# Start addresses of fp32r operands, moved off the common point of a 256-byte stretch

## The reference

```
# block 1 (blocks 2 and 3 have other branches and the same outline)
x = layer_norm(ALPHA * x + 0.5 * (silu(x @ w_gate) * (x @ w_up)) @ w_down)      # tags f1, f1d
proj = x @ w_in                                                              # q, k, v, z, xbc, gates
y_attn = attention(q, k, v) @ w_attn_branch                                   # a1_yh, a1_yl
y_ssm  = ssd(...) @ w_ssm_branch                                              # z1_yh, z1_yl
x = layer_norm(ALPHA * x + (gate_a * y_attn + gate_s * y_ssm) @ w_out)        # tag o1
x = layer_norm(ALPHA * x + 0.5 * swiglu(x, ffn2))                             # tags f2, f2d
# block 2: stick-breaking attention (a2), spatial gate (g2), gated linear attention (l2), o2, c2d
# block 3: sparse attention (a3), pools (p3), delta rule (d3), o3, f3 (first projection), f3d
```

## Time and profile before

| | us |
|---|---|
| median of 2 runs | 3423.38 (3421.72 and 3425.03) |
| the profiled execution: span from first to last instruction | 3420.3 |
| outside that span in the two runs (run less span) | 1.4 and 4.7 |
| TensorE busy | 3348.4 (98%), 18576 matmuls |
| VectorE busy | 2278.8 (67%) |
| ScalarE busy | 1593.4 (47%) |

### The profile page before, as it was taken

One profiled execution on the slowest core, in us unless ns is written; L12 is line 12 of the kernel. 1 busy time (PEld: TensorE's weight loads), 2 busy tenths in 40 slices (PEclk: granted clock), 3 DMA queues, 4 the chain that ended last, 5 costly groups with the idle time before them and its releaser, 6 DMA issues. The chain is left out here.

```text
span 3420.3 us, 48737 instructions
## 1 busy us (share of the span) xinstructions
PE 3348.4 (98%) x18576; PEld 2856.2 (84%) x18576; DVE 2278.8 (67%) x3709; ACT 1593.4 (47%) x2932; POOL 339.6 (10%) x375
## 2 busy tenths in 40 slices
PE   8999999999999999999999999999999999999999
PEld 7998888877788899887887888888787888889987
DVE  6887474778447787853565576667465567678865
ACT  3565254454433455555324363346355243355654
POOL 1000200022010100022010100000000104222200
PEclk9999999999999999999999999999999999999999
DMA  6346312220334435520454242245410330142464
GB/s 218 109 149 206 111 49 64 91 69 25 104 102 137 157 108 170 173 73 25 160 161 143 75 134 97 96 165 168 122 38 26 109 99 26 38 148 81 136 200 157
DMA packets 107988, 386.48 MB, mean 113 GB/s; under 512 B 12060, under 2 KB 14764, under 8 KB 107504
## 3 DMA queue, kind: packets, MB, share of 16 engines
q1 hardware_dynamic: 101088, 364.86, 32.6%
q0 software_dynamic: 4528, 16.43, 1.5%
q10 hardware_dynamic: 2144, 2.10, 0.2%
HBM read 379.13 MB, written 4.21 MB: 112 GB/s over the span
## 5 line engine op out<-in xcount | busy, mean ns | idle before, releaser
L445 DVE TENSOR_TENSOR w_low<-ring,w_high 128x1024 fp32r<-128x1024 f32 (+1 forms) x481 | 591.3, 1231 | 496.3 <-ACT w_high L433 490.6
L433 ACT ACTIVATE w_high<-ring 128x1024 fp32r<-128x1024 f32 (+1 forms) x481 | 485.0, 1010 | 491.8 <-PE bank L469 212.8
L469 PE MATMUL bank<-x_low,w_high 128*128 128x512 f32 (+1 forms) x1712 | 654.9, 388 | 19.5 <-DVE w_low L445 13.0
L469 PE MATMUL bank<-x_high,w_low 128*128 128x512 f32 (+1 forms) x1712 | 641.4, 380 | 0.0
L469 PE MATMUL bank<-x_high,w_high 128*128 128x512 f32 (+1 forms) x1712 | 417.8, 381 | 0.0
L469 PEld LDWEIGHTS bank<-x_low,w_high 128*128 128x128 f32 x1712 | 323.1, 189 | 82.4 <-issue 17.6
L469 PEld LDWEIGHTS bank<-x_high,w_low 128*128 128x128 f32 x1712 | 323.4, 189 | 56.9 <-issue 3.6
L469 PEld LDWEIGHTS bank<-x_high,w_high 128*128 128x128 f32 x1712 | 304.6, 189 | 59.1 <-issue 4.8
L738 PE MATMUL bank<-w_low,x_high 128*128 128x512 f32 (+1 forms) x384 | 145.6, 379 | 3.6 <-ACT z_z L2102 1.5
L740 PE MATMUL bank<-w_high,x_high 128*128 128x512 f32 (+1 forms) x384 | 143.5, 374 | 0.0
L739 PE MATMUL bank<-w_high,x_low 128*128 128x512 f32 (+1 forms) x384 | 143.5, 374 | 0.0
(11 more groups left out here) (821 smaller groups left out, 8215.0 us busy)
## 6 DMA issues: line engine op xcount, KB each, us to landing
ring<-in_W SPq DMA_DIRECT2D x686, 512.0 KB, 3.5
X<-in_x POOLq DMA_DIRECT2D x1, 2048.0 KB, 9.7
x_spill<-X POOLq DMA_DIRECT2D x1, 2048.0 KB, 8.2
X<-x_spill POOLq DMA_DIRECT2D x4, 512.0 KB, 3.5
ring<-in_W SPq DMA_DIRECT2D x4, 432.0 KB, 4.0
out<-X SPq DMA_DIRECT2D x3, 512.0 KB, 5.5
const<-in_consts POOLq DMA_DIRECT2D x1, 1133.0 KB, 10.6
f_hid<-in_xT ACTq DMA_DIRECT2D x4, 256.0 KB, 8.2
```

What stands on the lines that cost most here:

```text
L433: ac.activation(b.UH[u.place][:, 0:u.K * u.n], u.src(), ACT.Copy).then_inc(*b.split.act.up("high", i))
L445: dv.tensor_tensor(b.UL[u.place][:, 0:n], u.src(), b.UH[u.place][:, 0:n].bitcast(F32), SUB).then_inc(*b.split.dve.up("low", i))
L469: i = pe.matmul(out, w[:, k, c], v, start=n == 0 and q == 0, stop=last and q == 3 * K - 1)
```

## The change

It gives a `past` of its own to each of these tiles, and leaves all instructions, their order and their waits as they are. One element is 4 bytes, so `past=4` is 16 bytes.

- `cols` (column constants): three lines on, as `const`.
- `x_high` 4 elements on, `x_low` 8.
- Branch inputs: a1 12 and 20, z1 24 and 28 (with `m1_xs`, which has the same place, 24), a2 32 and 36, g2 40 and 44, l2 48 and 52, a3 56 and 60, p3 16 and 2, d3 48 and 6.
- Inputs of the second projections: a table `IN_PAST` with one value for each of a tag's tiles, from 4 to 60. f3d keeps 0.

Tiles behind a moved one are pushed back to their own point, so they stay at the same point of the stretch, 256 bytes further on at most steps.

```diff
--- before.py
+++ after.py
@@ -237,12 +237,12 @@
         self.cl, self.csize = const_layout()
         self.cx = {0: a.take("const", self.csize[0], past=3 * LINE)}
         self.colat, self.ncol = col_at()
-        self.colt = a.take("cols", self.ncol)
+        self.colt = a.take("cols", self.ncol, past=3 * LINE)
         self.MOD, self.GN, self.cond = a.take("MOD", 48), a.take("GN", 2, 8), a.take("cond", 8)
         self.small = a.take("small", 112)
         self.X = a.take("X", 4, 1024)
-        self.XH = a.take("x_high", 8, 512, dtype=F32R)
-        self.XL = a.take("x_low", 8, 512, dtype=F32R)
+        self.XH = a.take("x_high", 8, 512, dtype=F32R, past=4)
+        self.XL = a.take("x_low", 8, 512, dtype=F32R, past=8)
         self.UH = [a.take("w_high", SLOT, dtype=F32R) for _ in range(NU)]
         self.UL = [a.take("w_low", SLOT, dtype=F32R) for _ in range(NU)]
         self.units, self.unit_of, self.key_of, self.n_high, self.n_low = [], {}, [], 0, 0
@@ -755,7 +755,7 @@
     def __init__(self, b, area, tag, nk, src, units=4):
         self.tag, self.nk, self.src, self.n = tag, nk, src, units
         self.tail, self.more, self.added, self.begun = units, {}, [], False
-        self.H = [area.take(f"{tag}_in", 2, 256, dtype=F32R) for _ in range(units)]
+        self.H = [area.take(f"{tag}_in", 2, 256, dtype=F32R, past=p) for p in IN_PAST[tag][:units]]
 
     def used(self, g, i):
         p, k = i // self.nk, i % self.nk
@@ -858,6 +858,7 @@
         x.then_inc(*g.pe.up(d.tag, "part", i))
 
 
+IN_PAST = {"f1d": (4, 8, 12, 16), "o1": (24, 32, 40), "o2": (28, 56, 60), "o3": (36, 44, 52), "f2d": (20, 24, 28, 32), "c2d": (36, 40, 44, 48), "f3d": (0, 0, 0, 0)}
 THIRD = "third tile of tokens done"
 
 
@@ -1507,8 +1508,8 @@
         self.S = [a.take("a1_s", 2, 257) for _ in range(5)]
         self.PT = [a.take("a1_pt", 4, 128) for _ in range(3)]
         self.sm = [a.take("a1_sm", 16) for _ in range(5)]
-        self.YH = a.take("a1_yh", 8, 512, dtype=F32R)
-        self.YL = a.take("a1_yl", 8, 512, dtype=F32R)
+        self.YH = a.take("a1_yh", 8, 512, dtype=F32R, past=12)
+        self.YL = a.take("a1_yl", 8, 512, dtype=F32R, past=20)
         self.units = [(n, j) for n in range(4) for j in range(8)]
         self.ba = Branch(self.gb, "ba1", "w_in", OGA, "w_attn_branch", [[(64 * lo, 64), (64 * hi, 64)] for lo, hi in PAIRS1],
                          Halves(lambda k: self.YH[:, k, :], lambda k: self.YL[:, k, :]), self.merged,
@@ -1517,7 +1518,7 @@
         a = Area(b, at)
         self.gcv, self.gd = Group(b, "conv1"), Group(b, "ssd1")
         xs_at = a.at
-        self.XS = a.take("m1_xs", 4, 2048)
+        self.XS = a.take("m1_xs", 4, 2048, past=24)
         after_xs = a.at
         self.BT = a.take("m1_bt", 4, 512)
         self.CT = a.take("m1_ct", 4, 512)
@@ -1542,9 +1543,9 @@
         self.DT = a.take("m1_dt", 4, 32)
         self.ssd = [(c, g) for c in range(4) for g in range(4)]
         self.yx_at = xs_at
-        self.YXH = Area(b, xs_at).take("z1_yh", 4, 2048, dtype=F32R)
+        self.YXH = Area(b, xs_at).take("z1_yh", 4, 2048, dtype=F32R, past=24)
         a = Area(b, after_xs)
-        self.YXL = a.take("z1_yl", 4, 2048, dtype=F32R)
+        self.YXL = a.take("z1_yl", 4, 2048, dtype=F32R, past=28)
         self.gz = Group(b, "z1")
         self.zt = [a.take("z1_z", 512) for _ in range(2)]
         self.sq = [a.take("z1_sq", 512) for _ in range(2)]
@@ -2333,7 +2334,7 @@
         self.W1 = [a.take("a2_w", 1280) for _ in range(2)]
         self.sinc = a.take("a2_sinc", 128)
         self.nge, self.nones, self.neg, self.eye = (a.take(f"a2_{n}", 128, dtype=F32R) for n in ("nge", "nones", "neg", "eye"))
-        self.YAH, self.YAL = a.take("a2_yh", 4, 512, dtype=F32R), a.take("a2_yl", 4, 512, dtype=F32R)
+        self.YAH, self.YAL = a.take("a2_yh", 4, 512, dtype=F32R, past=32), a.take("a2_yl", 4, 512, dtype=F32R, past=36)
         rows4 = down_rows(4)
         self.ba = Branch(self.gb, "ba2", "w_in_2", 4112, "p_a_2", rows4, halves(self.YAH, self.YAL), self.merged,
                          [gates.take("ba2_gate", 512) for _ in range(5)], (), False)
@@ -2341,7 +2342,7 @@
         self.gg = Group(b, "spatial")
         self.U = a.take("g2_u", 4, 512)
         self.V = a.take("g2_v", 4, 512)
-        self.YBH, self.YBL = a.take("g2_yh", 4, 512, dtype=F32R), a.take("g2_yl", 4, 512, dtype=F32R)
+        self.YBH, self.YBL = a.take("g2_yh", 4, 512, dtype=F32R, past=40), a.take("g2_yl", 4, 512, dtype=F32R, past=44)
         self.WS = a.take("g2_w", 8, 128)
         self.GN = a.take("g2_norm", 2, 512)
         self.bb = Branch(self.gb, "bb2", "w_in_2", 5136, "p_b_2", rows4, halves(self.YBH, self.YBL), self.merged,
@@ -2366,7 +2367,7 @@
         a = Area(b, m2)
         self.AT = [a.take("l2_at", 2, 128) for _ in range(3)]
         self.sq = [a.take("l2_sq", 128) for _ in range(2)]
-        self.YCH, self.YCL = a.take("l2_yh", 4, 512, dtype=F32R), a.take("l2_yl", 4, 512, dtype=F32R)
+        self.YCH, self.YCL = a.take("l2_yh", 4, 512, dtype=F32R, past=48), a.take("l2_yl", 4, 512, dtype=F32R, past=52)
         self.bcr = Branch(self.gb, "bc2", "w_in_2", 6160, "p_c_2", rows4, halves(self.YCH, self.YCL), self.merged,
                           [a.take("bc2_gate", 512) for _ in range(4)], [a.take("bc2_part", 512) for _ in range(2)], True)
         ada.late(4, Area(b, FLOATS - LINE - 8 * 512))
@@ -3188,7 +3189,7 @@
         self.units = [(n, j, h, br) for n in range(4) for j in range(4)
                       for h, br in ((0, 1), (0, 2), (1, 1), (1, 2), (0, 0))]
         self.pairs = [[(64 * j, 64), (64 * (j + 4), 64)] for j in range(4)]
-        self.YAH, self.YAL = a.take("a3_yh", 4, 512, dtype=F32R), a.take("a3_yl", 4, 512, dtype=F32R)
+        self.YAH, self.YAL = a.take("a3_yh", 4, 512, dtype=F32R, past=56), a.take("a3_yl", 4, 512, dtype=F32R, past=60)
         self.bn = Branch(self.gb, "bn3", "w_in_3", 3872, "w_branch_nsa_3", self.pairs, halves(self.YAH, self.YAL), self.merged,
                          [a.take("bn3_gate", 512) for _ in range(8)], (), False, 8)
 
@@ -3206,7 +3207,7 @@
         self.pa = [a.take("p3_a", 528) for _ in range(2)]
         self.pb = [a.take("p3_b", 528) for _ in range(2)]
         self.pc = [a.take("p3_c", 528) for _ in range(2)]
-        self.YBH, self.YBL = a.take("p3_yh", 4, 512, dtype=F32R), a.take("p3_yl", 4, 512, dtype=F32R)
+        self.YBH, self.YBL = a.take("p3_yh", 4, 512, dtype=F32R, past=16), a.take("p3_yl", 4, 512, dtype=F32R, past=2)
         self.bp = Branch(self.gb, "bp3", "w_in_3", 4896, "w_branch_pool_3", rows4, halves(self.YBH, self.YBL), self.merged,
                          [a.take("bp3_gate", 512) for _ in range(4)], [a.take("bp3_part", 512) for _ in range(2)], True)
         self.sp = [a.take("d3_sp", 4, 4) for _ in range(3)]
@@ -3233,7 +3234,7 @@
         self.WT, self.OI = self.T1, self.U
         a = Area(b, m1)
         self.SZ = a.take("d3_z", 4, 512)
-        self.YCH, self.YCL = a.take("d3_yh", 4, 512, dtype=F32R), a.take("d3_yl", 4, 512, dtype=F32R)
+        self.YCH, self.YCL = a.take("d3_yh", 4, 512, dtype=F32R, past=48), a.take("d3_yl", 4, 512, dtype=F32R, past=6)
         self.sqz = [a.take("d3_sqz", 128) for _ in range(2)]
         self.gz = Group(b, "z3")
         self.bd = Branch(self.gb, "bd3", "w_in_3", 5920, "w_branch_dn_3", rows4, halves(self.YCH, self.YCL), self.merged,
```

## The result

| | median us | lowest and highest | runs |
|---|---|---|---|
| before | 3423.38 | 3421.72 to 3425.03 | 2 |
| after | 3458.46 | 3457.39 to 3459.53 | 2 |

The ratio is 1.0096, with an interval of 1.0075 to 1.0118. The changed kernel is about 35 us slower. That is inside the predicted range and within 2%, but seven times the +4.9 us of the sum.

What follows compares the result with a forecast made beforehand. The prediction took TensorE's distances between matmuls to bound the kernel. Its four parts summed to +4.9 us, which with the 3420.3 us span and 3.1 us for the runs gave 3428 us, range 3350 to 3492 us.

Steps and rivals of the forecast that it cites:

- What bounds the kernel: TensorE, busy 3348.4 of 3420.3 us: time is the sum of distances between matmuls, nothing else worth over about 20 us.
- The sum: Whole kernel: 9.4 - 0.8 - 2.2 - 1.5 = +4.9 us, giving 3428 us; chance 0.60.
- slower rival: Moving operands starting inside a line pay 6.6 ns, +55.5 us; stationary ones perhaps +21.9 us more; chance 0.22.
- part A: Turned tokens (`x_high`, `x_low`) as moving operand, 7260 matmuls at L469 and L647: 1.3 ns each, +9.4 us.
- part B: Turned tokens as stationary operand at L738 to L740, 1152 matmuls: -0.7 ns each, -0.8 us.
- C: Inputs of the second projections, stationary at L852 to L854, 2160 matmuls: half of a 2 ns gain, -2.2 us.
- D: Branch inputs as moving operand, 1152 matmuls: -1.3 ns each, -1.5 us.
- The faster rival: Operands with equal starts hinder each other, any distance helps: -6.5 ns on 11724 matmuls, -76 us, 3347 us; chance 0.15.
- The whole loss gone: All 13.3 ns lost per matmul vanish on 11724 matmuls: 156 us less, 3267 us; chance 0.03.
- No effect at all: TensorE's two independent read ports, one for each operand, would make the change worth exactly nothing.
- What the profile would show: x at L469, 512 columns: 396 to 406 ns; f3d stays 389 to 392; branch inputs show loss by point.
- line rival: Another name for the slower rival; at L469 with 512 columns it claimed 403 to 412 ns.

Runs made afterwards that it cites:

- e2: Only `x_high`, `x_low` and `cols` moved (to 4, 8 and 48 elements) against the kernel before: 3445.45 us, ratio 1.0064.
- m1: Computation left out: fp32r matmul streams over 256 start pairs, d being stationary start less moving start modulo 64 elements: 1833.09 us.
- e3: Only the inputs of the second projections moved, by the table IN_PAST, against the kernel before: 3432.26 us, ratio 1.0021.
- e4: Only the branch inputs moved (with `m1_xs`), against the kernel before: 3430.56 us, ratio 1.0021.
- e5: `x_high` and `x_low` one line (16 elements) on, `cols` three lines, against the kernel before: 3439.25 us, ratio 1.0045.
- e13: Against the kernel before: weights and f3d inputs at 4, x and branch inputs at 20, other second-projection inputs at 12: 3427.84 us, ratio 1.0007.
- e6: `x_high` and `x_low` three lines (48 elements) on, `cols` three lines, against the kernel before: 3444.34 us, ratio 1.0055.
- the sweep: Kernels without the computation, timing 16 moving by 16 stationary starts at 512 and 256 columns, in two orders: 1833.09 and 1835.27 us.
- e1: All large tiles, weights and inputs alike, 4 elements on, distances unchanged, against the kernel before: 3446.25 us, ratio 1.0067.
- m2: Same as m1 but with the stationary starts in descending order, so each stream has another predecessor: 1835.27 us.

## Why the prediction was right or wrong

**What bounds the kernel** was right: TensorE's distances are the time, the other engines and waits gave nothing (VectorE +3.2 us of busy time, the two waits no longer), and the edit acts by the pace of the matmuls alone. Not foreseen was that up to 5 us of waits might come back.

**The sum** was mis-sized. +4.9 us were forecast, 35 measured. That the time came inside the range says little for the working: the range ran some 70 us each way, past the slower rival's first step, and none of the four parts has the size that was forecast for it, so as far as the sum goes it is luck. The step that failed first is in **part A**: "a third of 4 ns, 1.3 ns", a price between two points a line apart, spread over all widths. At 512 columns x at 4 and 8 costs 4.9 ns a matmul, and at 256 it gains 1.1. With the waits that is +16.9 us (e2 as a whole, with part B: +20.7) in place of +9.4. The prediction named this as what would make it wrong, that the loss hangs on points finer than a line. It does: by steps of 4 elements, and between two points there is no slope: at 512 columns d = 4, 8 and 12 with a moving start 4 past a multiple of 8 are at 236.8, 226.7 and 229.9 ns in m1.

**Parts B, C and D** had the wrong sign. B and C were forecast by a third and a half of a difference seen at 256 columns (-0.7 and -1 ns), D by the middle between one seen at 256 and one at 512 (-1.3 ns), and what is seen at 256 does not carry over to 512. Measured: about +4, +5 and +5 ns, +4.3, +10.8 and +5.6 us (the last two by e3 and e4 alone +7.5 and +5.8). The d that is best for 256 columns gives 233.2 ns at 512. That the stationary operand's start counts as the moving one's does was not in the prediction, which took the earlier trace rows to speak against it.

**The slower rival** (line crossing) had the size of many a slower pair, 6.6 ns against 233.3 - 226.7, and the wrong reason; its whole, +55 or +77 us, was too much, since pairs differ and 256 columns lose nothing. e5 pays 15 us with all starts at a line's start, and e13 pays nothing that can be told with all starts inside one. That 6.6 ns is also 16 columns' time at 2.4 GHz, one line's, may be what made it look right.

**The faster rival** (distance helps) falls by e5, e6 and the sweep: distances of one and three lines cost 15 and 20 us, and at 512 columns distance 0 is already at the least pace, while by e1 the same distance with both starts at 4 costs 4 ns. What it read in the earlier trace rows is true, for 256 columns and d = 16.

**The whole loss gone** did not come: of 1024 streams in the two sweeps none is below 226.7 or 113.3 ns. The Trainium skill, "TensorE: Matmul & The Clock Gate", section "Back-to-back issue gap", has N/2.4 + 2.5 ns for what it calls the isolated gap of a single matmul, and an estimate from it is 215.8 ns for 512 columns. In this one-pass format the traces disagree, with 226.7 at the best.

**No effect at all** was what the prediction drew from two independent read ports. The Trainium skill, "TensorE: Matmul & The Clock Gate", section "Step-by-step: what each phase is for", gives TensorE one such port for each operand. The runs disagree with what was drawn from it, and more than the earlier trace rows did: the pace hangs on how the two operands' starts stand to each other, up to 10 ns. Whether the ports are at fault, no run shows.

**What the profile would show**: x at 512 columns was to be 396 to 406 ns if right and 403 to 412 by the line rival; 401 to 409 came, between them. f3d stayed where it was, as said. The branch inputs were to show the loss as a function of the point. Their high.high products show 394 to 398 ns, since most points are at a slow pace; the other products spread more, from 391 to 426 ns, and `l_yl` and `l_yh` with 426 and 415 had 420 and 419 before.

What stays open is the physical cause: what makes a period of 256 bytes in the distance and of 32 bytes in the place, and why a stream can settle at either of two paces. No run here looks inside.

No version that was run beats both kernels. For 512 columns the point of before is already near the least pace (227.7 against 226.7 ns), and e13 only equals it. At 256 columns, 2916 matmuls at 118.8 ns could by an estimate from the table gain 5.5 ns each, 16 us, if x and weights stood at d = 16 for them. The same tiles feed the 4368 matmuls of 512 columns. With a moving start at a multiple of 8 elements d = 16 costs 6.5 ns on each of those, but with one 4 past it the table has 228.9 ns at 512 columns, 2.2 ns or about 10 us in all, and 113.3 to 114.1 at 256. And moving 20, stationary 4, the pair of e13, is at 226.7 ns at 512 columns in both sweeps and at 113.3 at 256 in m2 (118.4 in m1). So a few us may be left for a kernel that places x, weights and units by both widths. It was not tried, nor were separate places for the two widths.

## What to carry to other kernels

Where fp32r matmuls bound a kernel, start addresses matter: a slow pair cost 3% of a matmul's time here, 4% in a few pairs, so sweep all pairs at the width in use before placing anything, in both orders. Do not interpolate between two measured starts, and do not carry a gain over from another width. Without a sweep, leave both operands at the same point modulo 256 bytes, at a multiple of 32 bytes: at 512 columns nothing was faster, and in the sweep five pairs in six had a slower pace. With 256 columns alone that is near the slowest choice, and d = 16 the fastest.

## What the runs showed of the hardware

- The least distance of one-pass fp32r matmuls is 17 cycles of 2.4 GHz for 16 columns: 226.67 ns = 512 x 17/16 / 2.4 and 113.33 ns for 256. Slower streams at 512 columns have means up to 236.9 ns (first streams aside), and many, 233.3, are 16 cycles above the least. Some are even (both at 4: steps of 230 to 232 ns), others repeat a pattern (moving 4, stationary 8: 239 and 234 or 235 in turn).
- In this sweep the pace goes by the distance of the operands' starts modulo 256 bytes and by the moving start modulo 32 bytes, 57 of 64 sets agreeing within 1.6 ns, and for some pairs (46 of 256 at 512 columns, first streams aside) also by something that changes with the order of the streams.
- The same pair can be the fastest at 512 columns and near the slowest at 256 (distance 0, multiple of 8: 226.7 where the table runs from 226.7 to 236.8, and 119.9 where it runs from 113.3 to 120.3).
- Single stretches of 3.4 or 6.8 us have the lower clock (0.51), one in the execution profiled before and three in the one after. Each 0.001 of mean clock goes with some 2 us. Over 62 runs of the kernel before, which took 3420.9 to 3430.0 us, that is a part of the scatter and not the whole: those at 0.997 alone span 3422.4 to 3430.0.
